# Gate blocks of the next tile in another order: memory queries and memory gates first, attention gates second

## What is computed

```python
z, q, k, v, q_idx, k_idx, w_idx = front(x, pos, g_pre, w_in)          # RMSNorm, one input projection
...
scores = indexer_scores(qib, wb, k_idx, valid)                        # 8 index heads, ReLU, weighted sum
_, sel = lax.top_k(scores, n_sel)                                     # 256 keys for each query
att = attend_selected(qb, k_sel, v_sel, sel <= tb[None, :, None])     # 8 heads
...
mo = mem_attend(z["q_mem"], mk, mv)                                   # 4 heads, 256 memory tokens
...
o = jnp.concatenate([att * jax.nn.silu(z["g_att"]),
                     conv * jax.nn.silu(z["g_conv"]),
                     mo * jax.nn.silu(z["g_mem"])], axis=-1) @ w_out
return x + rms_norm(o, g_post)
```

## Time and profile before

| what | value |
|---|---|
| median of three executions | 2413.73 us (2400.1 to 2415.58) |
| profiled execution, its own time | 2410.6 us |
| profiled execution, span from first to last instruction | 2408.8 us |
| around the span | 1.8 us |
| mean granted TensorE clock | 0.90 of 2.4 GHz |
| DMA over the span | 60 GB/s on average |

### The profile page before, as it was taken

One profiled execution on the slowest core, in us unless ns is written; L12 is line 12 of the kernel. 1 busy time (PEld: TensorE's weight loads), 2 busy tenths in 40 slices (PEclk: granted clock), 3 DMA queues, 4 the chain that ended last, 5 costly groups with the idle time before them and its releaser, 6 DMA issues. The chain is left out here.

```text
span 2408.8 us, 33367 instructions
## 1 busy us (share of the span) xinstructions
PE 2116.4 (88%) x12592; PEld 1698.6 (71%) x12592; DVE 1404.0 (58%) x3150; ACT 1200.8 (50%) x2337; POOL 113.5 (5%) x174
## 2 busy tenths in 40 slices
PE   7999999989996889889999878999989989979765
PEld 4776676767765767666778658786777868759662
DVE  2334775676643565657866755697576352625680
ACT  1102467777741346466666765566656675422000
POOL 0000000000000000000000000000000000010004
PEclk9999999999996789989999997999988898977556
DMA  7213121221114212120211010110110001032001
GB/s 277 78 52 104 61 75 63 71 69 61 47 48 154 98 48 66 54 67 12 73 59 57 20 58 33 38 53 8 54 42 20 27 21 45 29 135 85 1 4 33
DMA packets 61888, 144.57 MB, mean 60 GB/s; under 512 B 14288, under 2 KB 28536, under 8 KB 60704
## 3 DMA queue, kind: packets, MB, share of 16 engines
q1 hardware_dynamic: 59552, 131.95, 16.5%
q0 software_dynamic: 2176, 10.49, 1.3%
HBM read 100.18 MB, written 42.24 MB: 59 GB/s over the span
## 5 line engine op out<-in xcount | busy, mean ns | idle before, releaser
L1576 PE MATMUL psum<-sb_v,sb_ptb 128*128 128x64 f32 x2176 | 323.0, 296 | 35.3 <-ACT sb_ptb L1179 34.5
L1576 PEld LDWEIGHTS psum<-sb_v,sb_ptb 128*128 128x128 f32 x2176 | 309.5, 218 | 48.8 <-ACT sb_ptb L1179 48.1
L817 PE MATMUL psum<-sb_w,sb_xt 128*128 128x512 f32 (+5 forms) x1088 | 333.9, 463 | 0.5 <-DVE sb_xt L550 0.5
L1179 ACT ACTIVATE sb_ptb<-psum 128x512 f32<-128x512 f32 (+3 forms) x352 | 183.2, 536 | 225.3 <-PE psum L1568 221.2
L817 PEld LDWEIGHTS psum<-sb_w,sb_xt 128*128 128x128 f32 (+1 forms) x1088 | 180.8, 187 | 125.5 <-issue 113.2
L1568 PE MATMUL psum<-sb_con,sb_p 128*128 128x128 f32 x1280 | 222.6, 298 | 49.7 <-ACT sb_p L1198 36.2
L1351 DVE CUSTOM_DVE_ANT_0 sb_p<-psum,sb_bias 128x1024 f32<-128x1024 f32 (+7 forms) x128 | 126.7, 990 | 203.0 <-PE psum L1558 162.7
L856 PE MATMUL psum<-sb_xt,sb_w 128*128 128x128 f32 x2048 | 237.3, 276 | 0.0
L856 PEld LDWEIGHTS psum<-sb_xt,sb_w 128*128 128x128 f32 x2048 | 234.3, 192 | 1.1
L1600 PE MATMUL psum<-sb_wo,sb_mix 128*128 128x512 f32 x512 | 231.9, 596 | 0.0
L295 ACT ACTIVATE sb_lowj<-sb_sc,sb_l_ncand,sb_l_scl 128x1152 bf16<-128x1152 f32 (+7 forms) x128 | 219.7, 1717 | 4.1 <-DVE sb_l_step L256 2.1
(11 more groups left out here) (408 smaller groups left out, 2953.6 us busy)
## 6 DMA issues: line engine op xcount, KB each, us to landing
qt_s<-sb_qt SPq DMA_DIRECT2D x32, 512.0 KB, 2.9
sb_x<-in_x_prompt SPq DMA_DIRECT2D x16, 512.0 KB, 4.6
xt_s<-sb_xt SPq DMA_DIRECT2D x16, 512.0 KB, 2.6
sb_qa<-qt_s SPq DMA_DIRECT2D x16, 512.0 KB, 4.4
sb_qa<-qt_s SPq DMA_DIRECT2D x32, 256.0 KB, 5.8
sb_xres<-in_x_prompt SPq DMA_DIRECT2D x16, 512.0 KB, 4.4
out_y_prompt<-sb_y SPq DMA_DIRECT2D x16, 512.0 KB, 3.0
sb_p<-xt_s SPq DMA_DIRECT2D x9, 512.0 KB, 5.7
```

What stands on the lines that cost most here:

```text
L817: mm = pe.matmul(out, m.xt[:, p, k, 0:n], m.w1[:, k, lo:hi], start=(k == 0), stop=(k == KD - 1))
L1179: act.activation(m.ptb[:, g, 0:cols], m.turn[slot][:, 0:cols], ACT.Copy).then_inc(s.t_act, 1)
L1576: mm = pe.matmul(o, m.ptb[:, g, x * P:(x + 1) * P], v, start=st, stop=sp)
```

## The change

The eight gate blocks are computed in the order 4, 5, 6, 7, 0, 1, 2, 3 instead of 0 to 7. The index products keep their places. Everything that follows from this moves along: ACT's copy of the memory queries and its tanh of the memory gates stand after step 1, and its tanh of the attention gates after step 3. DVE's two multiplies change places in the same way. The planner's list, the semaphore counts and ACT's waits for `gated` and `y_sq` are adapted. PE's memory scores now wait for `zact` at 3j+1, which is the copy.

```diff
--- before.py
+++ after.py
@@ -1047,7 +1047,7 @@
                     turns.append((("to", j), "t_dve"))
         scores += products(j, range(-1, 8))
         if j + 1 < NT:
-            turns += [(("z", j + 1, x), "t_dve") for x in range(2)]
+            turns += [(("z", j + 1, x), "t_dve") for x in (1, 0)]
             scores.append((("M", j + 1), "mem_exp"))
         if j >= 0:
             turns.append((("ta", j), "t_dve"))
@@ -1218,11 +1218,11 @@
         gate = m.gate[:, j % 2, :]
         act.wait_ge(s.t_done, n)
         if x == 0:
-            if j >= 2:
-                act.wait_ge(s.gated, j - 1)
-                act.wait_ge(s.y_sq, j - 1)
             act.activation(gate[:, 0:512], m.turn[slot][:], ACT.Tanh, scale=0.5).then_inc(s.zact, 1)
             return
+        if j >= 2:
+            act.wait_ge(s.gated, j - 1)
+            act.wait_ge(s.y_sq, j - 1)
         if j >= 1:
             act.wait_ge(s.t_done, turns.of[("to", j - 1)][1])
         act.activation(m.qm[:], m.turn[slot][:, 0:256], ACT.Copy).then_inc(s.zact, 1)
@@ -1251,9 +1251,9 @@
             relus(j, x)
             if j + 1 < NT:
                 if x == 1:
+                    gates(j + 1, 1)
+                if x == 3:
                     gates(j + 1, 0)
-                if x == 3:
-                    gates(j + 1, 1)
                     memory(j + 1)
             if j >= 0 and x == 5:
                 take_y(j, 1)
@@ -1419,7 +1419,7 @@
 
         slot = turns.of[("z", j, x)][0]
         gate = m.gate[:, j % 2, :]
-        dve.wait_ge(s.zact, 3 * j + 1 + 2 * x)
+        dve.wait_ge(s.zact, 3 * j + 3 - x)
         lo, hi = ((0, 512), (512, 768))[x]
         dve.scalar_tensor_tensor(out=gate[:, lo:hi], in0=gate[:, lo:hi], scalar=1.0,
                                  in1=m.turn[slot][:, 512 - hi + lo if x else 0:512], op0=ALU.add,
@@ -1546,7 +1546,7 @@
                            m.xt2(j)[:, k, :], start=(k == 0), stop=(k == KD - 1))
         if b % 4 == 3:
             mm.then_inc(s.z2_done, 1)
-            pe.wait_ge(s.z2_done, 2 * j + b // 4 + 1)
+            pe.wait_ge(s.z2_done, 2 * j + 2 - b // 4)
             pe.sem_inc(s.t_done, 1)
 
     def scores_of(j, h):
@@ -1585,7 +1585,7 @@
     def memory(j):
 
         slot = slot_of(scores, ("M", j))
-        pe.wait_ge(s.zact, 3 * j + 2)
+        pe.wait_ge(s.zact, 3 * j + 1)
         for h in range(NMH):
             e = slice(64 * (h % 2), 64 * (h % 2) + 64)
             mm = pe.matmul(m.score2(slot)[:, mem_at(h) * 256:][:, 0:256], m.qm[e, (h // 2) * P:(h // 2 + 1) * P],
@@ -1608,10 +1608,10 @@
         products(j, -1)
         if j + 1 < NT:
             pe.wait_ge(s.xt2_ld, 16 * (j + 2))
-        for b in range(8):
+        for n, b in enumerate((4, 5, 6, 7, 0, 1, 2, 3)):
             if j + 1 < NT:
                 gate_block(j + 1, b)
-            products(j, b)
+            products(j, n)
         if j + 1 < NT:
             memory(j + 1)
         if j >= 0:
```

## The result

The changed kernel takes 2398.82 us, the median of 20 runs (2388.15 to 2418.07), beside 2415.43 us for the kernel before, also 20 runs. The ratio is 0.9941, with a 95% interval of 0.992 to 0.9962. So it is faster by 0.4 to 0.8%, some 14 us. The forecast was 6.5 us (2407), with a range of its own from 2403 to 2411 and a wider one from 2396 to 2420 that takes in the rivals. The measured median lies in the wider one only.

A forecast was written before the change was run, and what follows sets the result against it. PE was taken to lead, with 17.7 us of waits for ACT's copy removable. Gains of 5.8 us by DVE and ACT and 7.2 by PE gave 6.5, so 2413.7 - 6.5, or 2407, range 2403 to 2411, wider 2396 to 2420.

The forecast's parts named there:

- What bounds the kernel and what the wait can give: PE leads stage B; its wait for ACT's memory-query copy, 17.7 us in 16 tails, is all that can be gained.
- Residual wait: Tails without index products: PE still waits 0.15 us for its own last block, so it gains 0.51 of 0.66 us.
- The chain account: Gain passed on by DVE and ACT in the tails: 3.1 + 0.8 + 1.6 + 0.3 = 5.8 us.
- The other bound of the prediction: DVE's idle time ahead of L1459, 12.0 us in 14 tails, 8.1 after the wider multiply, caps the DVE and ACT gain.
- Index tails: the gain is mostly lost at product 9: Tails with index products: DVE's chain moves only 0.26 us, six tails give 1.6; product 9 waits 1.87 us in tile 0.
- Sum: All tails: 5.8 us by DVE and ACT, 7.2 by PE; 6.5 taken.
- The clock: Around the removed waits the granted clock shows 1.00, so removing them gives back no clock.
- The whole wait back: All of PE's wait in the tails is gained, 16.5 us, giving 2397; chance 0.12.
- nothing reaches the end: Earlier tails only wait longer for ACT in the head parts, time stays 2413.7 us; chance 0.20.
- The third: Long PE waits at product 9 lower the clock, 2.2 us each; in all seven tails 9 us slower, 2422.6; chance 0.08.
- The signs named: L1591's wait under 0.2 us, L1459 idle about 0.4 or near 0, product 9 waiting 1.2 to 3, no 0.50 clock there.
- The stage: Stage B, 1396 us: the forecast is wrong if it shrinks by more than 12 us or not at all.

The follow-up runs named there:

- maxima first: Changed kernel with DVE taking the memory maxima ahead of gating the attention result; 2375.98 and 2385.01 us in two sets, ratios 0.9844 and 0.9849.
- the repeats: Kernel before and changed kernel, each run again unedited; 2415.11 us (ratio 1.0009) and 2404.36 us (ratio 0.9945).
- the experiment on single kinds of tails: Kernel before with the new order only in tails with index products, 2414.73 us (1.0002), or only in the others, 2402.25 us (0.9958).
- the one with the maxima ahead of both gates: Changed kernel with DVE taking the memory maxima ahead of gating the attention result and of its last gate multiply; 2398.74 us, ratio 0.9917.
- the trace with the filler: Changed kernel with eight 128x256 matmuls, result unread, added in PE's wait at the head of tile 9; 2399.52 us, ratio 0.9955.

## Why the prediction was right, and where it was off

**What bounds the kernel and what the wait can give.** Right. The wait for the copy went away in every tail, and with the wait put back the time went back.

**Residual wait.** 0.15 us was taken from the gap between two halves of blocks, 0.30 was measured. There the gap stood between two blocks; here the next matmul is the memory scores. The gain per tail without index products is 0.36 in tail 8, not 0.51, and 8 x 0.15 = 1.2 us of the sum for PE is missing for that reason (seven tails and the one of tile 1). Idle time ahead of L1459 was to be about 0.4 in such tails and is 0.62 in tail 8, since, counted from the start of the second half of the blocks, the multiply starts 0.06 earlier (1417.05 - 1408.91 against 1417.03 - 1408.83) and PE comes 0.15 later than computed. The chain account had the same error. The other bound of the prediction, 12.0 us in 14 tails, took in the 1.21 us of the last tile's tail, which the change can't touch; it is 10.8 in 13, and 7.2 in place of 8.1 after the wider multiply.

**Index tails: the gain is mostly lost at product 9.** Right, and shown from three sides: the grown wait (13.1 us), the kernel with the order in these tails only (2.3 us of 11.1), and maxima first, which shortens DVE's part of the chain and gets 7.5 us out. But more is lost than was computed. The forecast for tile 0 was a wait of 1.87 and it is 2.03; the seven are 1.45 to 2.73, inside the 1.2 to 3 given. Of the 0.16 us too much, 0.11 is a handover on DVE: L1424 ends at 849.06 and L1459 starts at 849.17, where the prediction let one start as the other ended. Of the 0.26 us that such a tail should gain some 0.1 is left by product 9's account (1.48 - 2.03 + 0.65), and as much by the start of L1459 in the other tails of this kind. So this term is 6 x 0.1 = 0.6 us in the trace, where 1.6 was forecast.

**Sum.** By waits, 6.5 was forecast (5.8 to 7.2); PE's account of waits in the trace gives 5.0, and at equal clock the runs give 8.0 ± 0.6. The two kinds of tails split the way that was computed: 2.3 ± 0.9 in the index tails (forecast 1.6 + 0.3) and 4.9 ± 0.8 in the others (forecast 3.1 + 0.8 by the chain, 3.6 + 1.8 by PE). The sum was therefore right to about 1.5 us. But part of that is luck. Read from the rows, the chain gained about 6 x 0.36 + 0.75 + 0.6 + 0.4 = 3.9 us where 5.8 was computed (0.75 is the tail of tile 1, 0.4 the first one, each from the end of its gate part to L1459 or the maxima). Both accounts of the trace, 3.9 and 5.0, lie under the forecast and the 8.0 of the runs over it. Those 3 us are not explained by the waits of PE that the change touches. Nor does the sum of all its waits settle it: 277.6 us before and 273.3 changed, 275.7 and 275.0 in the repeats. ACT's wait for `sb_mnb`, said to change hardly, went from 63.2 to 59.9 us.

**The clock.** This is the largest term that the prediction left out. It costed it at nothing: removed waits give back no clock, because the windows behind them show 1.00. Measured are some 4 us in favour of the change, half of the 8.0 at equal clock, at two standard errors. The rows behind the removed waits were read correctly, but the mean over the program is not set there: the low stretches lie elsewhere, as those behind 1445.10 above, and they differ between executions of one kernel (1480 to 1510 has a clock of 0.60 in the first trace of the changed kernel and 0.89 in its second). That part of the forecast could not have come out of these rows, and its cause is not found. Of the 8.4 us between the forecast's 2407.2 and the median of 2398.8, 4 are this clock and 1.5 the gain at equal clock; the rest is within the spread of medians. The time lies outside the 2403 to 2411 that the mechanism was given, and inside the wider range, which was drawn for the rivals and the spread. That it lies there says little for the mechanism; the experiments do.

**Rivals.** The whole wait back (2397) lies close to the median, and is false all the same. Product 9 took 9.7 us of it, and the index tails, with 11.1 of the 17.7 us, give 2.3. At equal clock the gain is 8.0 and not 16.5. Without the experiment on single kinds of tails the median alone would have spoken for it. That nothing reaches the end falls by both sets of the changed kernel. The third, a clock that falls at product 9, was said to decide only from waits near 3.48 us. That is wrong: a low clock stood behind waits of 1.91 to 2.73, in one of three such tails per trace. Its price was right in size (1.7 against 2.2 us; the window of the earlier trace rows begins 0.64 us inside the wait) and it strikes once and not seven times, so it took a quarter of the gain at most and not all.

**The signs named.** A clock of 0.50 at product 9 was to speak against the forecast, and it was seen, at 854 to 856 in the first trace. It costs too little to overturn it. The stage gave no verdict: from the first index product to the first instruction of stage C it takes 1393.2 us before and 1398.7 changed in the first pair of traces, 1399.9 and 1389.9 in the repeats. The other signs came as said, but for the 0.30 us of L1591, where under 0.2 was named, and the 0.54 to 0.62 us ahead of L1459, where about 0.4 was.

## What to carry to other kernels

A wait of the busiest engine is worth what is left when the next wait on the same path has taken its share. So follow the path to the next place where that engine looks for the result, and add up the other engine's chain in front of it. Inside an engine that works strictly in its order, put first what another engine waits for: on DVE the memory maxima ahead of the gating, two instructions of 1.23 and 0.69 us swapped, were worth 12.2 us at equal clock where the reordering on three engines was worth 8.0. And where executions differ in granted clock, compare at equal clock before a cause is named, and by the measured time before a version is chosen; here the two gave different winners.

## What the runs showed that was not expected

- The spread between executions of one kernel, 30 us here, is almost all granted clock: 2.04 us per 0.001, and what is left once it is taken out is 2.5 us (20 runs of the changed kernel).
- Kernels with the same instructions get different clocks: 0.907 and 0.905 in two sets of maxima first, 0.897 in the kernel before and in the one with the maxima ahead of both gates. Between the best two that is 18 us, more than any single edit here was worth. Why is open.
- A stretch of PE at over 90% busy can stand at the lower level for long: in the changed kernel's trace 1480 to 1515 has 32.71 us of work in 35 at a clock of 0.66, and at the same place in the trace with the filler it is 1.00. The kernel before has it too, with 21.48 us of work in the 22 from 1486 to 1508 at 0.50.
- A wait of PE for its own last block cost 0.30 us ahead of the memory scores and 0.15 between two halves of gate blocks.
